# An inference step of a hybrid decoder: the B1 weight load without two of its waits, and another order of the SyncE queue between attention and retention

## The reference, cut to what matters

```python
h = rms_norm(x, norm_g); p = h @ w_in                  # 1024 -> 3328 columns
A: sliding-window attention with sinks (window 128, 8 heads, 2 kv heads, head dim 64)
B: retention, 4 heads of 128 x 128, chunks of 128 tokens, a state carried from chunk to chunk
x = x + concat(silu(gA) * A, silu(gB) * rms_norm(B)) @ w_out
```

## Time and profile before

| | us |
|---|---|
| three runs, median | 1928.33 |
| lowest, highest | 1925.64, 1941.27 |
| the profiled execution | 1925.64 |
| its span | 1923.8 |

### The profile page before, as it was taken

How to read it: one execution, slowest core, us unless ns; L and a number is a source line. 1 busy time by engine, 2 the same in 40 slices (tenths; PEclk the granted TensorE clock), 3 DMA queues, 4 the chain that set the end, 5 groups by cost and what they waited for, 6 DMA issues and landing times.

```text
span 1923.8 us, 35859 instructions
## 1 busy us (share of the span) xinstructions
PE 1790.1 (93%) x11752; PEld 989.6 (51%) x11752; DVE 1385.0 (72%) x4744; ACT 721.9 (38%) x1841; POOL 68.5 (4%) x108
## 2 busy tenths in 40 slices
PE   0778899999999999978998999999999999999999
PEld 0345555655555555533444655555555555555444
DVE  4769999977665766678885899998766576667442
ACT  2556576631232222232443556664123222222010
POOL 3010000010000000021001000000100000000000
PEclk9899999999999999989999999999999999999999
DMA  5874545463002100089994333335400021004875
GB/s 151 205 188 72 99 94 109 82 155 118 11 11 102 64 9 11 16 211 248 248 238 133 57 77 73 72 79 107 141 12 11 28 93 54 11 11 129 199 203 157
DMA packets 353806, 196.66 MB, mean 102 GB/s; under 512 B 296624, under 2 KB 327536, under 8 KB 353552
## 3 DMA queue, kind: packets, MB, share of 16 engines
q1 hardware_dynamic: 343984, 159.89, 35.5%
q0 software_dynamic: 9728, 35.66, 5.7%
HBM read 88.75 MB, written 41.16 MB: 68 GB/s over the span
## 4 chain that ended last, share of the span: by engine, by line
PE 58%; DVE 22%; DMA 6%; ACT 4%; issue 4%; SPq 2%; DVEq 0%; ACTq 0%; POOL 0%
PE PB L514 23%; PE PA L514 23%; DVE r L1060 2%; DMA r<-r 2%; DVE r L1017 2%; PE S L668 2%; PE OB L687 2%; PE TK L657 2%; PE S L703 1%; DVE mix L1135 1%; PE OB L694 1%; DVE r L1022 1%; DVE w_mx L871 1%; DMA out<-r 1%; ACT w_a L1727 1%
## 5 line engine op out<-in xcount | busy, mean ns | idle before, releaser
L514 PE MATMUL PB<-w_a,hT 128*128 128x512 f16 (+1 forms) x1920 | 404.4, 361 | 0.0
L514 PE MATMUL PA<-w_a,hT 128*128 128x512 f16 (+1 forms) x1920 | 403.0, 360 | 1.0 <-DVE land L1003 1.0
L514 PEld LDWEIGHTS PB<-w_a,hT 128*128 (+1 forms) x1920 | 185.7, 99 | 178.5 <-issue 11.8
L514 PEld LDWEIGHTS PA<-w_a,hT 128*128 (+1 forms) x1920 | 186.1, 99 | 171.4 <-issue 3.8
L514 PE MATMUL PA<-w_b,r 128*128 128x512 f16 x768 | 172.9, 382 | 20.4 <-DMA r<-r 15.3
L1799 ACT ACTIVATE r<-OB 128x128 f32<-128x128 f32 (+1 forms) x136 | 36.3, 272 | 390.7 <-PE S L703 364.2
L514 PE MATMUL PA<-w_b,hT 128*128 128x512 f16 x768 | 179.6, 384 | 0.0
L514 PE MATMUL PB<-w_b,hT 128*128 128x512 f16 x768 | 176.3, 379 | 0.6 <-DVE r L1162 0.6
L514 PE MATMUL PB<-w_b,r 128*128 128x512 f16 x768 | 171.3, 379 | 0.9 <-DVE r L1284 0.9
L1182 DVE TENSOR_TENSOR r<-S,t_dec 128x256 f32<-128x256 f32 x64 | 27.2, 425 | 156.1 <-PE S L668 155.9
L514 PEld LDWEIGHTS PA<-w_b,r 128*128 128x128 f16 x768 | 74.5, 98 | 115.0 <-DMA r<-r 20.5
(11 more groups left out here) (258 smaller groups left out, 2894.3 us busy)
## 6 DMA issues: line engine op xcount, KB each, us to landing
out<-r SPq DMA_DIRECT2D x40, 512.0 KB, 4.7
r<-mixed SPq DMA_DIRECT2D x32, 512.0 KB, 4.1
w_b<-in_w_in POOLq DMA_DIRECT2D x16, 512.0 KB, 8.8
mixed<-mix SPq DMA_DIRECT2D x32, 256.0 KB, 2.0
mixed<-mix SPq DMA_DIRECT2D x64, 128.0 KB, 1.8
w_a<-in_w_in POOLq DMA_DIRECT2D x16, 512.0 KB, 8.0
w_b<-in_w_out POOLq DMA_DIRECT2D x16, 512.0 KB, 7.1
r<-in_x_prompt SPq DMA_DIRECT2D x16, 512.0 KB, 4.6
```

Source lines behind the costliest of these rows:

```text
L514: last = nc.tensor.matmul(out[0:s.rows, 0:n], lhs, w16(ph, k, p, wpart), start=(k == 0 and part == 0 and wpart == 0), stop=(k == KT - 1 an ...
```

## The change

Three edits. POOL drops its waits on `a_tp` and `sts_ld` ahead of the B1 load, in both layers. On SP the stores of `nk_p` and `nv_p` move behind the store of E and behind `load_states("B0")`, in both layers. In layer 0 the four cache copies move from B0 (after the stores of T0 and T1) to between the store of E and `load_states`.

```diff
@@ POOL, layer()
                         pool.wait_ge(dve_piece, free)
-                        if kind == "B1":
-                            for g in range(2):
-                                pool.wait_ge(a_tp[g], 16 * (L + 1) * TILES)
-                            pool.wait_ge(sts_ld, (L * 2 + 1) * 32)
                         load_weights(G, kind, nl)
@@ SP, layer()
                 prob_T(L, E - 1, 1)
                 prob_T(L, E, 0)
+                store_mix("A", L, E - 1)
+                prob_T(L, E, 1)
+                store_mix("A", L, E)
+                if L == 0:
+                    for o, i in ((nk_s, cache_k), (nv_s, cache_v)):
+                        for l in range(DEPTH):
+                            sp.dma_start(o[l, :, 0:WINDOW - DEC_SEQ].rearrange("b w g d -> b (w g d)"),
+                                         i[l, :, DEC_SEQ:WINDOW].rearrange("b w g d -> b (w g d)")).then_inc(kc_out, 16)
+                for g in range(2):
+                    sp.wait_ge(a_tp[g], 16 * (L + 1) * TILES)
+                load_states("B0", L)
                 for o, c0 in ((nk_p, A_W), (nv_p, A_W + KV_W)):
                     sp.dma_start(at(o).rearrange("o n w g d -> (o n w) (g d)"),
                                  land[:, E.par, c0:c0 + KV_W]).then_inc(kv_out, 16)
-                store_mix("A", L, E - 1)
-                prob_T(L, E, 1)
-                store_mix("A", L, E)
-                for g in range(2):
-                    sp.wait_ge(a_tp[g], 16 * (L + 1) * TILES)
-                load_states("B0", L)
                 if not last:
                     load_gains(L + 1)
@@ SP, B0 and B1
                     store_mix(ph, L, T1)
-                    if ph == "B0" and L == 0:
-                        (the same four cache copies)
                     for h in range(2):
```

## The result

The changed kernel takes 1990.32 us (median of 4 runs, 1988.82 to 1991.69) against 1928.85 us for the kernel before on the same chip (4 runs, 1925.64 to 1941.27). The ratio is 1.0306 with a 95% interval of 1.0261 to 1.0353. That is 61.5 us slower between the medians (59 by the ratio), where the prediction had 34. It lies above the range as well. The profiled execution of the changed kernel took 1986.21 us.

The account below looks back on a forecast made before the run. TensorE, busy 93% of the span, was taken as the bound. Delays of 16.4 + 7.1 (stores), 5.5 + 5.5 (transposes) and 1.8 (clock) made 36.3 us on 1925.6, stated as 1962 us; range 1942 to 1979.

Parts of the forecast that it names:

- the stores of keys and values: Head of B0: ScalarE's first step waits for the moved stores to land, 16.4 us late in layer 0, 7.1 in layer 1.
- The copies' part: Layer 0, head of B0: cache copies on half the DMA engines stand ahead of states and stores; 8.1 us for the copies.
- the rival of early stores: Head of B0: small stores overtake copies and states, delays 9.9 and 6.1 us; 1953 us, or 1942 with harmless transposes; chance 0.10.
- the copies spread over 16 engines: Layer 0, head of B0: alternative to copies on 8 engines; the stores' delay would be 14.2 us, not 16.4.
- the transposes, +5.5 us in each layer: Transposes of E-1 beside the early B1 load land in 9.9 us, not 4.4, delaying TensorE; bounds 1 and 13.
- Equal turns in time: Transposes of E-1: engines alternating equally between queues would add some 2.8 us a layer, making the total 5.4 us less.
- The transposes wait for the whole load: Rival at the transposes of E-1: 13 us a layer in place of 5.5, 1977 us; chance 0.13.
- the clock: After the new stalls TensorE's matmuls run at the 1.2 GHz level: 1.8 us for layer 1, nothing for layer 0.
- Costs nothing: B1 load's earlier start gains nothing, its first reader never waited; earlier last transpose of E and moved copies also cost nothing.

## Why the prediction was wrong

**Right: what happens, where, and in which order.** It is slower, by both mechanisms named. GpSimd's L485 starts at the last gate, the transposes land late, L1060 stands idle, and L1775 is released by `out<-land`.

**Right in size: the stores of keys and values.** Predicted 16.4 and 7.1 us, measured 16.8 and 7.7 in the changed kernel, 17.2 and 7.9 with SyncE's order alone. The copies' part was 16.4 - 7.1 = 9.3, and the kernels with and without them differ by 9.4. The stores landed as late as a queue kept in order makes them, so the rival of early stores fell. With the copies spread over 16 engines the layer 0 term would have been 14.2, further from the 16.8. In the changed kernel the share is 0.66 at 436 us and jumps to 1.03 when the states come in beside the copies, then falls to 0.47 and 0.20; that fits copies on half of the engines only roughly.

The place of the wait was wrong in layer 0, all the same. The sum had the last store leave SyncE 6.2 us after the store of E and wait in the DMA queue for another 9.9. In the changed kernel it leaves some 13 us after the store of E, because the states take 6.42 us to issue in place of 2.21 and the two stores 3.46 in place of 2.41. Then the two land 4.1 us (their median) after issue, nearly as fast as the 3.4 of before. So most of the wait is in front of the issue and not behind it. That the total still came out within 0.4 us is in part luck. Layer 1 went nearly as the sum says.

**Wrong: the transposes, +5.5 us in each layer.** This is the step that failed. They cost 15.2 and 18.4 us, 33.6 together where 11.0 was in the sum, and the upper bound of 13 was too low as well. With the measured values in its place, 16.4 + 7.1 + 33.6 = 57.1, where the spans differ by 60.6. The step went wrong in three ways:

- *The row was not like the case.* The 9.9 us came from transposes in block O with two weight rows beside them. I wrote that here there are eight and did not scale. The runs with 2, 4 and 8 rows show that the wait grows with each.
- *The turns of the queues were read as turns of equal time.* Equal turns in time would double a transpose, the prediction says. Its sum went by the rows and not by this. Equal turns in packets make it 9 times slower while they last, which comes to waiting for nearly all of the load. Neither packet size nor packet count was in the rows I had chosen, and both were there to be had from the trace of before: 3283 packets of 250 bytes in one place, 397 of 3.6 KB in the other. With their durations (1.12 x 64 / 3283 = 0.022 us and 1.027 x 64 / 397 = 0.166 us) a factor of (0.022 + 0.166) / 0.022 = 8.5 could have been worked out blind.
- *The rival with the right mechanism got too small a price and chance.* "The transposes wait for the whole load" stood at 13 us a layer, 1977 us, chance 0.13. Its mechanism is the one that held, nearly, but the load isn't over after its own 12.2 us. The first transpose lands 19.5 us after issue in layer 0, where the load's and its own time alone are 12.2 + 4.4 = 16.6. In part the transposes take their turns as well. In part the DMA engines moved less: 211 GB/s at 398 to 402 us, against 352 at 402 to 406, and why is open.

**Wrong in sign: the clock.** I added 1.8 us for a second spell at the 1.2 GHz level. The granted clock does fall in the new stalls, but the spell of before, 4.44 and 4.45 us for twelve matmuls in place of 2.75, has gone in both layers: 3.4 us less, and not 1.8 more.

**Costs nothing: right, with a margin that is now known.** The weights were ready early in the kernel before, and 5.95 us of wait in their first reader still cost nothing. The load had no need to be earlier.

## What to carry to other kernels

Before a large load is moved up, look at what else is in flight on the DMA engines at that moment and who waits for it. Compare the packet sizes of the two queues: if the engines take one packet of each in turn, as they did here for 8 us, the queue with small packets is slowed by the ratio of a whole round to its own packet, for as long as the other has work. A wait that looks useless on a prefetch may be what keeps it off a transfer with no slack. And a small store whose completion frees a buffer belongs ahead of large transfers of the same queue, or its landing is theirs.

## What was not expected of the hardware

- DMA transposes move in packets of about 250 bytes. Beside GpSimd's load of 3.7 KB packets they fall from 3283 packets in 4 us to 359. Beside ScalarE's 1 KB packets they get 777.
- Issue slows down too, not only landing. The two transposes took SyncE 4.09 us before and 18.50 beside the load. The two issues of the states took SyncE 2.21 us before and 6.42 behind the copies, and the five last rows of the load took ScalarE 12.27 us, where GpSimd issues eight in 5.98. Why they differ isn't settled by these runs.
- The granted clock fell to 0.50 in the stall at 440 us, with TensorE idle since 435 us.
